# The downward projection of the inner MLP chunks as seven block products, each added by one VectorE instruction over four banks

## What is computed

```
def squared_relu_mlp(x, w_up, w_down):
    return jnp.square(jax.nn.relu(x @ w_up)) @ w_down
...
        xp = layer_norm(ALPHA * xp + squared_relu_mlp(xp, mlp_w_up[i], mlp_w_down[i]), ln2_g[i], ln2_b[i])
```

## Time and profile before

| | |
|---|---|
| median of 3 runs | 1091.1 us (1089.22 to 1091.69) |
| the profiled execution | 1089.57 us, of it the span in the trace 1087.7 us |
| TensorE matmuls | 1072.9 us busy (99%), 8535 instructions |
| VectorE | 749.5 us busy (69%), 1239 instructions |
| ScalarE | 564.1 us busy (52%), 1003 instructions |
| GpSimd | 194.5 us busy (18%), 247 instructions |
| DMA | 136.42 MB, mean 125 GB/s |

### The profile page before, as it was taken

One profiled execution on the slowest core, in us unless ns is written; L12 is line 12 of the kernel. 1 busy time (PEld: TensorE's weight loads), 2 busy tenths in 40 slices (PEclk: granted clock), 3 DMA queues, 4 the chain that ended last, 5 costly groups with the idle time before them and its releaser, 6 DMA issues.

```text
span 1087.7 us, 22255 instructions
## 1 busy us (share of the span) xinstructions
PE 1072.9 (99%) x8535; PEld 1052.9 (97%) x8535; DVE 749.5 (69%) x1239; ACT 564.1 (52%) x1003; POOL 194.5 (18%) x247
## 2 busy tenths in 40 slices
PE   8999999999999999999999999999999999999996
PEld 8999999999999999999999878999999999999996
DVE  6999999785646657466874664887856556466566
ACT  6999857652432424324666775675432424324233
POOL 2111032001101011012244564300101011010023
PEclk9999999999999999999999999999999999999998
DMA  7323306365848558462141220162858558484202
GB/s 253 113 88 97 111 27 193 60 192 132 216 126 187 169 106 219 111 216 92 27 130 45 77 61 20 59 175 48 229 137 189 172 109 215 126 187 136 78 2 83
DMA packets 53598, 136.42 MB, mean 125 GB/s; under 512 B 5536, under 2 KB 21344, under 8 KB 53504
## 3 DMA queue, kind: packets, MB, share of 16 engines
q1 hardware_dynamic: 44192, 101.10, 28.4%
q0 software_dynamic: 9040, 33.67, 17.2%
q10 hardware_dynamic: 288, 0.59, 0.1%
HBM read 132.81 MB, written 3.56 MB: 125 GB/s over the span
## 4 chain that ended last, share of the span: by engine, by line
PE 92%; DVE 2%; ACT 2%; issue 1%; POOL 1%; DMA 1%; SPq 0%; DVEq 0%; POOLq 0%; ACTq 0%
PE bank L2002 13%; PE bank L2003 13%; PE bank L2004 13%; PE bank L2258 8%; PE bank L2260 8%; PE bank L2259 8%; PE bank L2232 6%; PE bank L2234 6%; PE bank L2233 6%; PE bank L2089 2%; PE bank L2091 2%; PE bank L2090 2%; PE bank L2393 1%; PE bank L2367 1%; PE bank L2411 1%
## 5 line engine op out<-in xcount | busy, mean ns | idle before, releaser
L1164 DVE TENSOR_TENSOR w_lo<-stage,w_hi 128x1024 fp32r<-128x1024 f32 x108 | 130.7, 1221 | 83.5 <-ACT w_hi L681 83.5
L2002 PE MATMUL bank<-x_hi,w_hi 128*128 128x288 f32 (+1 forms) x560 | 163.3, 292 | 2.1 <-DVE w_lo L1157 1.2
L2003 PE MATMUL bank<-m_lo,w_hi 128*128 128x288 f32 (+1 forms) x560 | 162.2, 290 | 0.0
L2003 PE MATMUL bank<-x_lo,w_hi 128*128 128x288 f32 (+1 forms) x560 | 161.7, 289 | 0.0
L2004 PE MATMUL bank<-m_hi,w_lo 128*128 128x288 f32 (+1 forms) x560 | 161.6, 289 | 0.0
L2002 PE MATMUL bank<-m_hi,w_hi 128*128 128x288 f32 (+1 forms) x560 | 161.6, 289 | 0.0
L2004 PE MATMUL bank<-x_hi,w_lo 128*128 128x288 f32 (+1 forms) x560 | 160.9, 287 | 0.0
L681 ACT ACTIVATE w_hi<-stage 128x1024 fp32r<-128x1024 f32 x108 | 110.3, 1053 | 81.3 <-DMA stage<-w_up 61.0
L2232 PE MATMUL bank<-m_hi,w_hi 128*128 128x288 f32 (+1 forms) x512 | 147.7, 288 | 0.3 <-DVE w_lo L1157 0.3
L2234 PE MATMUL bank<-m_hi,w_lo 128*128 128x288 f32 (+1 forms) x512 | 147.6, 288 | 0.0
L2233 PE MATMUL bank<-m_lo,w_hi 128*128 128x288 f32 (+1 forms) x512 | 147.4, 288 | 0.0
(11 more groups left out here) (283 smaller groups left out, 2798.3 us busy)
## 6 DMA issues: line engine op xcount, KB each, us to landing
stage<-w_up SPq DMA_DIRECT2D x64, 512.0 KB, 5.7
stage<-w_down SPq DMA_DIRECT2D x64, 512.0 KB, 3.7
t_raw<-w_up POOLq DMA_DIRECT2D x36, 512.0 KB, 5.6
stage<-w_up POOLq DMA_DIRECT2D x24, 512.0 KB, 7.8
t_raw<-w_up SPq DMA_DIRECT2D x12, 512.0 KB, 3.6
stage<-w_qkv SPq DMA_DIRECT2D x10, 512.0 KB, 3.9
stage<-w_x SPq DMA_DIRECT2D x8, 512.0 KB, 5.4
stage<-w_y SPq DMA_DIRECT2D x8, 512.0 KB, 3.4
```

Of the source, the lines that this page charges most:

```text
L1164: vt.tensor_tensor(lo, raw, hi.bitcast(F32), ALU.subtract).then_inc(s_wlo, 1)
L2002: mm(out, wh, xh, start=(k == 0), stop=False)
L2003: mm(out, wh, xl, start=False, stop=False)
```

## The change

The down projection of the inner chunks is also done by seven block products. `w_down` is taken as four blocks, two along the contraction by two along the output, and each block product has four output tiles by two rows of contraction: again 24 matmuls. The names of the fourteen weight blocks of a chunk are U11, UT1, UT2, U21, UT3, UT4, U22 (up) and D11, DT1, DT2, D22, DT3, D21, DT4 (down), and TensorE runs them in this order. T stands for a combination. DT1, DT2 and DT4 are built one after the other in the buffer of D11, DT3 in that of D22, and UT1, UT2, UT4 in that of U11, by DMAs that add. The hidden side needs seven parts: H11, H12, H22 and the combinations S1, S2, S3, S4, each with a rounded part and a rest.

The kernel works with four buffers `stage`; `t1_raw` is gone. Buffers are shared as follows: U11, UT1, UT2, UT4 one; U22, UT3, D22, DT3 one; D11, DT1, DT2, DT4 one; U21, D21 one. A chunk has fourteen splits in place of eleven, six loads and eight adds in place of nine loads and five adds. The products alternate between banks 0 to 3 and banks 4 to 7; when a product is done, one VectorE instruction adds its four banks to `acc` (or subtracts them), 4x256 or 4x288 columns.

ReLU and squares move from VectorE (one instruction a block) to ScalarE (a ReLU and one or two squares a block). The core of the diff:

```diff
+            def settle(l, c, i, j):
+                b0 = turned(l, (0, 4, 0, 4, 0, 4, 0)[j])
+                m = (0, 4, 4, 4, 4, 0, 0)[j]
+                c0, n = HALF[(0, 1, 0, 0, 1, 0, 1)[j]]
+                a = acc[:, m:m + 4, c0:c0 + n]
+                dve.wait_ge(*pair_done(l, c, j, 1, i))
...
+                vt.tensor_tensor(a, a, bank[:, b0:b0 + 4, 0:n], ALU.subtract if j in (2, 4) else ALU.add)\
+                    .then_inc(s_acc, 2)
...
             def chunk_down(l, c, i=0):
-                for m in range(4):
-                    accumulate(l, c, 0, m, i)
-                split_in(l, c + 1, B11, i)
...
+                settle(l, c, i, 0)
+                part_lo(l, c, i, S2)
+                part_lo(l, c, i, H12, 4)
...
+                part_sum(h12[:, :, :], h12[:, :, :], h22[:, :, 0:256], ALU.add)
...
+                    split_in(l, c + 1, U11, i)
+                part_lo(l, c, i, S4)
+                settle(l, c, i, 1)
+                part_sum(h21[:, :, :], h11[:, :, :], h21[:, :, :], ALU.subtract)
+                split_in(l, c, DT3, i)
+                settle(l, c, i, 2)
+                part_lo(l, c, i, S3)
+                split_in(l, c, DT4, i)
+                settle(l, c, i, 3)
...
+                    split_in(l, c + 1, U22, i)
+                split_in(l, c, D21, i)
```

SyncE's list, where the next chunk's U22 is loaded:

```diff
+                bring(l, c + 1, U22, s_yin, up_block(l, c + 1, 1, 1, i), split_done(l, c, DT3, i))
```

GpSimd's list at the start of a layer:

```diff
+                up_sum(l, 1, UT1, 0, 1, s_ux, (s_xu, 16 * (6 * l + 1)))
+                up_sum(l, 1, UT3, 0, 1, s_uy, split_done(l, 1, U22))
+                up_sum(l, 1, UT2, 1, 1, s_ux, split_done(l, 1, UT1))
```

TensorE's down products:

```diff
+                down_product(l, c, i, D11, H11, 0, True, drained)
+                down_product(l, c, i, DT1, S1, 4, True,
+                             lambda p: (combined(l, c, 3, i) if p else kept(l, c, 7, i),))
+                down_product(l, c, i, DT2, S2, 0, False, again(0))
+                down_product(l, c, i, D22, S4, 4, False, again(1))
+                down_product(l, c, i, DT3, S3, 0, False, again(2))
+                down_product(l, c, i, D21, H12, 4, True, again(3))
+                down_product(l, c, i, DT4, H22, 0, False, again(4))
```

More of the change, by code:

```diff
@@ L76 @@
 BANKS = 8
+H11, H22, S1, S2, H12, S4, S3 = range(7)
+HIDDEN_WIDTH = {H11: 256, H12: 256, S4: 256, H22: HW, S1: HW, S2: HW, S3: HW}
+ROUND_ORDER = (H11, H22, S1, H12, S2, S4, S3)
+REST_ORDER = (H11, H22, S1, S2, H12, S4, S3)
+U11, UT1, UT2, U21, UT3, UT4, U22 = UP = tuple(range(7))
+D11, DT1, DT2, D22, DT3, D21, DT4 = DOWN = tuple(range(7, 14))
+PLACE = {U11: 0, D11: 0, UT1: 1, DT1: 1, U22: 2, DT2: 2, UT2: 3, D22: 3, U21: 4, DT3: 4, UT3: 5, D21: 5, UT4: 6, DT4: 6}
+BEFORE = {k: o for k in PLACE for o in PLACE if PLACE[k] == PLACE[o] and k != o}
+FIRST = (U11, UT1, U22, UT2, U21, UT3)
+AROUND = ((UT2, 0), (D11, 0), (UT4, 0), (D22, 0), (DT1, 0), (DT2, 0), (U11, 1), (DT3, 0), (DT4, 0), (U22, 1), (D21, 0),
+          (UT1, 1), (U21, 1), (UT3, 1))
+SPLITS = len(AROUND)
 def build(nc, xp_t, xs_t, vec, w_y, w_x, w_ga, w_gi, w_out, w_qkv, w_o, w_up, w_down,
@@ new lines, in raw_ready @@
+        def raw_ready(l, c, k, i=0):
+            n = before(l, c)
+            if (c, k) == (1, U11):
+                return s_xd, 16 * (7 * l + 1)
+            on, each, base = {U11: (s_xu, 16, 16 * (6 * l + c)), D11: (s_xd, 16, 16 * (7 * l + c + 1)),
+                              U22: (s_yin, 32, 32 * n + 16), D22: (s_yin, 32, 32 * n + 32),
+                              U21: (s_zin, 32, 32 * n + 16), D21: (s_zin, 32, 32 * n + 32),
+                              UT1: (s_ux, 48, 48 * n + 16), UT2: (s_ux, 48, 48 * n + 32), UT4: (s_ux, 48, 48 * n + 48),
+                              DT1: (s_dx, 48, 48 * n + 16), DT2: (s_dx, 48, 48 * n + 32), DT4: (s_dx, 48, 48 * n + 48),
+                              UT3: (s_uy, 16, 16 * n + 16), DT3: (s_dy, 16, 16 * n + 16)}[k]
+            return on, i * each + base
@@ L957, in next_weights @@
[L957 to L962 removed]
+                split_in(l, c, UT4, i)
+                split_in(l, c, D22, i)
+                split_in(l, c, DT1, i)
+                keep(l, c, i, 4, 0, 4, h22[:, 0, :], -1.0)
+                rectify(l, c, i, low, 1)
```

678 lines of the change are left out of this document (354 added, 324 removed).

## The result

The changed kernel takes 1162.7 us (median of 4 runs, 1159.41 to 1166.18), the kernel before 1090.2 beside it: a ratio of 1.0665, with a 95% interval of 1.0626 to 1.0703. The prediction was 1131.8 us with a range of 1106 to 1155. The direction was right; the loss is 72.5 us where 40.7 were forecast, and the time lies outside the range. The profiled execution took 1166.18 us, its span is 1164.4.

What follows compares the result with a forecast made beforehand. TensorE's columns were taken as the bound; with new waits, a layer was 59.0 + 4 x 46.8 + 47.3 = 293.3 us, +20.3, two layers +40.7 on 1089.6, plus 1.5 for the median: 1131.8 us, range 1106 to 1155.

Steps and rivals of the forecast that it cites:

- What TensorE saves: Inner chunks, down projection as seven products: 42.66 us of TensorE work a chunk, 2.83 less; 34.0 us over twelve chunks.
- The price of an add over four banks: VectorE's adds of products to acc: 1.22 and 1.35 us by width, taking banks to cost nothing.
- the loop's stops ahead of D22, DT3 and D21: Looped chunk: TensorE waits about 1.0, 0.8 and 2.2 us there.
- the stop ahead of UT2: First inner chunk of a layer: TensorE stops 6.8 us, as UT2's add is issued behind UT3's, which waits for U22's split.
- VectorE's load (33 us): Inner chunk: VectorE has about 33 us of work in 42.7.
- Rival 1: VectorE's share decides, not its order: TensorE stays without a pause, 1057 us, faster; chance 0.06.
- the adds by DMA were taken to be in time: Looped chunk: an add takes 5.4 us, queued ones 3.0 each; UT4's copy just in time, about 0.1 us stop at DT2.
- such a delay for UT4 (1.9 us): Looped chunk: if an add took 3.4 us in the queue, UT4 would start 1.9 us later.
- rival 3: DMA and clock: eight adds put transfers over 3.4 us apart, or TensorE's clock falls after long stops; 1155 to 1175; chance 0.12.
- my end for "long": Upper bound with adds 3.4 us apart: looped chunk 48.65, first 60.8, last 49.0; 1154 us in all.
- The first and last inner chunks: Each layer: first 59.0 us, with stops ahead of UT2, UT3 and UT4; last 47.3, with 2.8 ahead of chunk 7.
- The list from E+4.8: Looped chunk: VectorE's unbroken queue from S2's combination of h12 to DT3's split, ending E+15.0; E is UT4's end.

Runs made afterwards that it cites:

- v1_half_adds: The changed kernel's work in another order, with each DMA add moving only 512 of 1024 columns: 1081.7 us, ratio 0.993 to the kernel before.
- x1_ut2_first: Changed kernel with UT2's add issued ahead of UT3's at the start of each layer: 1153.5 us, ratio 1.058 to the kernel before.
- x3_half_adds: Changed kernel with each DMA add moving only 512 of a block's 1024 columns: 1128.9 us, ratio 1.036 to the kernel before.
- x7_plain_loads: Changed kernel with GpSimd's DMAs overwriting the buffer in place of adding to it: 1128.6 us, ratio 1.037 to the kernel before.
- x2_filler: Changed kernel with 48 extra matmuls ahead of UT2 and 24 ahead of UT4 in each layer's chunk 1, results thrown away: 1169.7 us, ratio 1.074.

## Why the prediction was wrong, step by step

**Right.** What TensorE saves: a loop chunk of v1_half_adds takes 43.8 us with 0.9 of stops and 0.3 lost between matmuls, which leaves the forecast's 42.6. The price of an add over four banks; the place of the loop's stops ahead of D22, DT3 and D21 and their sum within 0.4 us; the mechanism and size of the stop ahead of UT2 (6.8 and 6.2, forecast 6.8), which x1_ut2_first removed; VectorE's load (33 us). Rival 1 falls, since its condition (D21's weights in time) wasn't met.

**The step that failed: the adds by DMA were taken to be in time.** The sum let every add of the loop land in time, but for 0.1 us at DT2; rows for that it had only from a kernel with five adds in a chunk. Measured are stops of 0.4 us ahead of UT2, 0.6 ahead of UT4 and 1.2 ahead of DT2, all of them gone in x3_half_adds and x7_plain_loads, and 49.7 us a loop chunk, where the same transfers without adding give 46.2: 3.5 us. The forecast of 46.8 was nearly right for adds in time. The price of one add wasn't the mistake. "An add takes 5.4 us ... 3.0 us each when they queue" still holds (last section); but of the 95 adds in the trace 46 were issued while another was in flight, and others ran beside loads, so the medians are 5.5 and 6.5. For DT2's in the chunk shown the forecast's own prices give a landing at 354.6 (5.4 + 3.0 behind 346.19), when ScalarE had been free for it since 353.7. By this estimate they hold about half of its wait; the rest is that DT3's add ahead of it took 6.6 us. The prediction priced such a delay for UT4 (1.9 us), but only outside its sum.

Eight loop chunks by 2.9 us over the forecast are 23 of the 36 us by which the two profiled executions differ more than forecast (76.6 for 40.7). That is near rival 3's first half, to which I gave, with the clock, 0.12; but its condition, adds more than 3.4 us apart, is not what happened to adds that queued closely, and my end for "long" (48.65 us a loop chunk) lay below.

**The clock: put at nothing.** Rival 3 named it and priced a product at the low clock at about 3 us. It fell after some four in ten of the stops of about 2 us, and after nearly all longer ones. In the changed kernel's two layers about 14 us are lost between matmuls beyond what an undisturbed chunk loses (0.45 us). How much of it could be had is open: x2_filler got nothing back, but its extra work held up UT4 itself.

**The first and last inner chunks: nearly right.** 61.5 and 60.2 for 59.0; the stops were less than forecast (14.1 and 12.9 for 16.3), of them 3.8 and 3.6 ahead of UT4 for 3.1, but only 0.5 and 0.2 ahead of UT3 for 2.1; the clock took about 4. That the totals came so near is in part luck. The last ones took 49.6 and 48.4 for 47.3, with a stop of 3.3 ahead of chunk 7 for 2.8 in layer 0. Around the inner chunks another 5 us were lost, which no term held.

**Slips in the working.** The list from E+4.8 adds up to E+15.1, not 15.0; TensorE wants D22 at E+12.1 and DT1's add ends at E+13.2, which gives the stop of about 1.0 and not "3.2 us before"; 59.0 + 4 x 46.8 + 47.3 is 293.5, not 293.3. Together they move the forecast by less than 2 us.

**Too narrow a range.** The bounds moved hand-offs and adds by a few tenths. The page of the kernel before already had adds with a median of 7.8 us from issue to landing, in a kernel where TensorE never waited for them. The change raised the adds to eight and let more products hang on them; there the range should have gone further.

## What to carry to other kernels

When work is moved into DMAs that add, count them at what such a DMA costs when several are queued, and draw their chain with the engine that splits their result: here plain transfers gave back 34 of the 72 us and a better order 65, and the two overlap. Stops along one chain don't add up: the last late operand takes in what the others give back, so find that operand's chain before anything else is shortened. And before a change of this kind is dropped, its order is worth another pass: 65 of the 72 us lay in the order of the same instructions.
